# Host-packed weight loads, and low parts of the down weights on POOL with its own walk over the experts

## The reference, cut to what matters

```python
a = RMSNorm(h); proj = a @ w_in               # z | x,B,C | dt | u,v
h += concat(ssd(z, xBC, dt), gmlp(u, v)) @ w_out
h += HierMoE(RMSNorm(h))                      # the best of 4 groups, then the best 2 of its 4 experts
h += sigmoid(RMSNorm(h) @ w_pg) * RMSNorm(p @ w_ple)
y = RMSNorm(h)

# HierMoE, for each expert e of 16 (1024 -> 512 -> 1024):
hid = silu(t @ w_gate[e]) * (t @ w_up[e])
y = y + comb[:, e:e+1] * (hid @ w_down[e])
```

## Time and profile before

| | |
|---|---|
| median of three runs | 1130.89 us |
| the profiled execution | 1131.93 us |
| its span, from the first to the last instruction | 1130.1 us |
| PE busy | 1057.6 us, 94% |
| DVE busy | 700.2 us, 62% |
| ACT busy | 502.7 us, 44% |
| POOL busy | 184.1 us, 16% |
| moved by DMA | 204.82 MB, mean 181 GB/s |

### The profile page before, as it was taken

One profiled execution on the slowest core, in us unless ns is written; L12 is line 12 of the kernel. 1 busy time (PEld: TensorE's weight loads), 2 busy tenths in 40 slices (PEclk: granted clock), 3 DMA queues, 4 the chain that ended last, 5 costly groups with the idle time before them and its releaser, 6 DMA issues.

```text
span 1130.1 us, 17444 instructions
## 1 busy us (share of the span) xinstructions
PE 1057.6 (94%) x6221; PEld 912.5 (81%) x6222; DVE 700.2 (62%) x1103; ACT 502.7 (44%) x872; POOL 184.1 (16%) x344
## 2 busy tenths in 40 slices
PE   7999999997999999946999999799999999999896
PEld 5777799985776788745988999798899999878685
DVE  4422575814767667156599467889946753585664
ACT  6733322123111121151589357788935652564332
POOL 3611001100133112111000000000000000065542
PEclk9999999999899999857999999999999999999999
DMA  9701400222512362169399775999977556142441
GB/s 335 233 23 55 170 2 1 75 79 72 164 70 76 120 234 85 56 195 296 141 367 380 266 278 179 381 358 369 380 265 278 181 190 225 53 171 75 169 149 56
DMA packets 131607, 204.82 MB, mean 181 GB/s; under 512 B 11375, under 2 KB 98031, under 8 KB 131434
## 3 DMA queue, kind: packets, MB, share of 16 engines
q1 hardware_dynamic: 121450, 169.82, 44.2%
q0 software_dynamic: 6512, 21.77, 5.4%
q10 hardware_dynamic: 3600, 12.62, 2.8%
HBM read 169.74 MB, written 34.46 MB: 181 GB/s over the span
## 4 chain that ended last, share of the span: by engine, by line
PE 56%; DVE 10%; issue 4%; DMA 3%; ACT 2%; DVEq 1%; POOL 0%; ACTq 0%; SPq 0%; POOLq 0%; another core or an unknown queue 0%
PE bank L608 12%; PE bank L610 11%; PE bank L609 11%; PE bank L602 4%; DVE w_lo L1531 3%; PE bank L852 3%; PE bank L854 3%; PE bank L853 3%; PE bank L596 2%; PE bank L824 1%; PE bank L791 1%; DMA raw_gu<-in_w_up 1%; ACT w_hi L1923 1%; DMA xg<-m_rows,index_u 1%; DMA hx<-h_rows 1%
## 5 line engine op out<-in xcount | busy, mean ns | idle before, releaser
L608 PE MATMUL bank<-w_hi,xh 128*128 128x256 f32 x768 | 220.2, 287 | 2.7 <-DVE xl L1052 2.7
L609 PE MATMUL bank<-w_lo,xh 128*128 128x256 f32 x768 | 218.0, 284 | 0.0
L610 PE MATMUL bank<-w_hi,xl 128*128 128x256 f32 x768 | 218.0, 284 | 0.0
L1531 DVE SCALAR_TENSOR_TENSOR w_lo<-raw_gu,cols,w_hi 128x512 fp32r<-128x512 f32 x264 | 177.9, 746 | 10.9 <-ACT w_hi L1923 9.8
L1923 ACT ACTIVATE w_hi<-raw_gu,cols 128x512 fp32r<-128x512 f32 x264 | 165.4, 714 | 32.1 <-PE bank L610 16.4
L608 PEld LDWEIGHTS bank<-w_hi,xh 128*128 128x128 f32 x768 | 147.7, 192 | 4.2 <-issue 3.1
L609 PEld LDWEIGHTS bank<-w_lo,xh 128*128 128x128 f32 x768 | 147.9, 193 | 0.8
L610 PEld LDWEIGHTS bank<-w_hi,xl 128*128 128x128 f32 x768 | 147.7, 192 | 0.0
L608 PE MATMUL bank<-w_hi,hid_hi 128*128 128x512 f32 x192 | 79.6, 415 | 0.0
L2231 POOL COPY index_u<-token_u 128x1 uint32 (+1 forms) x25 | 6.1, 244 | 434.2 <-PE bank L602 411.5
L609 PE MATMUL bank<-w_lo,hid_hi 128*128 128x512 f32 x192 | 75.9, 395 | 0.0
(11 more groups left out here) (373 smaller groups left out, 2169.2 us busy)
## 6 DMA issues: line engine op xcount, KB each, us to landing
raw_gu<-in_w_gate SPq DMA_DIRECT2D x32, 1024.0 KB, 7.6
raw_gu<-in_w_up SPq DMA_DIRECT2D x32, 1024.0 KB, 10.1
raw_d<-in_w_down SPq DMA_DIRECT2D x16, 2048.0 KB, 11.8
y_rows<-yb ACTq DMA_DIRECT2D x24, 512.0 KB, 6.3
raw_w<-in_w_in SPq DMA_DIRECT2D x20, 512.0 KB, 6.3
xr<-in_x_prompt_t SPq DMA_DIRECT2D x8, 512.0 KB, 9.4
xst<-in_x_prompt SPq DMA_DIRECT2D x8, 512.0 KB, 9.7
raw_o<-in_w_out SPq DMA_DIRECT2D x8, 512.0 KB, 3.5
```

The costliest lines, as they stand in the source:

```text
L608: nc.tensor.matmul(out, lh(k), rh(k), start=(k == 0), stop=False)
L609: nc.tensor.matmul(out, lh(k), rl(k), start=False, stop=False)
L610: last = nc.tensor.matmul(out, ll(k), rh(k), start=False, stop=(k == (K or len(ks)) - 1))
L1531: ins = V.scalar_tensor_tensor(out=gu_lo[:, k, :, cols_], in0=raw_gu[q // KC][:, k, :, :], scalar=gain(e, k), in1=gu_hi[:, k, :, cols_].bi ...
```

## The change

Five things are changed.

- The host lays the weights out in the order of the buffers. w_in is loaded in runs of 4 KB, gate and up as four quarters of 1 MB in runs of 8 KB, down as two halves of 1 MB in runs of 8 KB. ACT waits for each quarter or half instead of each half or the whole.
- The low parts of the down weights are made by POOL, four passes (`d_low`), counted by the semaphore d_split. PE waits for d_split by halves, and `hid_transposes(1)` goes behind the first quarter of the down products.
- POOL walks the experts by `each_block`: in each block it gathers the next rows, and in a block with splits it then runs `d_low` of the next expert.
- The low parts of the second half of w_out are made by POOL (semaphore o_low); ACT's `decay(0)` comes after the first of its four high passes of that half.
- The fill with ones covers the 16 blocks that may be unused, always, and is issued right after the third w_in block's loads; the loads of p_in and ple_row come before the wait for the plan, that of ps_in before the loop over the experts.

The core of the diff:

```diff
@@ SP
+            for b in range(NE, BLOCKS):
+                sp.dma_start(y_rows[b * P:(b + 1) * P, :].rearrange("p (k n) -> p k n", n=P),
+                             ones[:, :].unsqueeze(1).to_broadcast([P, KC, P])).then_inc(s("unused_filled"), 16)
...
+                sp.dma_start(raw_gu[q][:, part * KC // 2:(part + 1) * KC // 2].rearrange("p k w n -> p (k w n)"),
+                             i["w_gate_up"][bass.ds(e, 1), q, part].rearrange("o p n -> p (o n)")).then_inc(s(f"w{2 * q + part}_loaded"), 16)
...
             def next_expert(e):
-                done = sp.snap(STEPS * e)
-                gate_up(e, 0, sp.snap(done - KC - DC))
-                gate_up(e, 1, sp.snap(done - DC))
-                down(e, done)
+                done = sp.snap(GU_STEPS * e)
+                for q in range(2):
+                    for part in range(2):
+                        gate_up(e, q, part, sp.snap(done - (3 - 2 * q - part) * KC // 2))
+                down(e, 0, sp.snap(DC * e - DC // 2))
+                down(e, 1, sp.snap(DC * e))
@@ PE, one_block
                 b_rows(pe.snap(16 * n + 16))
-                hid_transposes(1, pe.snap(2 * n + 1))
-                pe.wait_ge(s("w_split"), steps + STEPS)
+                pe.wait_ge(s("d_split"), d_steps + DC // 2)
...
                 for quarter in range(4):
                     part, half = quarter // 2, quarter % 2
+                    if quarter == 2:
+                        pe.wait_ge(s("d_split"), d_steps + DC)
+                    if quarter == 1:
+                        hid_transposes(1, pe.snap(2 * n + 1))
@@ DVE
             front(0)
-            for j in range(KC // 2):
-                o_split(1, j)
             weights(0)
...
-                if more and splits:
-                    split(e + 1, "D0")
                 if more:
                     b_hid(dve.snap(n + 1), 0)
-                if more and splits:
-                    split(e + 1, "D1")
@@ POOL
+            for j in range(KC // 2):
+                pool.wait_ge(s("a_high"), KC * 5 + KC // 2 + j + 1)
+                G.tensor_tensor(wo_lo[1][:, j, :], raw_o[:, j, :], wo_hi[1][:, j, :].bitcast(F32), ALU.subtract).then_inc(s("o_low"), 1)
...
-            gather(0, None, None)
-            total = blocks_in_all(pool)
-            with pool.Fori(0, total) as b:
+            def d_low(e):
+
+                done = STEPS * e if isinstance(e, int) else pool.snap(STEPS * e)
+                for k in range(DC):
+                    pool.wait_ge(s("w_high"), done + 2 * KC + k + 1)
+                    G.tensor_tensor(d_lo[:, k, :], raw_d[:, k, :], d_hi[:, k, :].bitcast(F32), ALU.subtract).then_inc(s("d_split"), 1)
+
+            def one_block(b, e, splits, more):
+
                 n = pool.snap(b + 1)
                 gather(n, n, pool.snap(16 * n))
+                if splits and more:
+                    d_low(e + 1)
+
+            gather(0, None, None)
+            d_low(0)
+            each_block(pool, one_block)
```

More of the change, by code:

```diff
@@ L61, in build @@
     TILES = NT + 1
-    IN = i["w_in"].shape[2]
+    IN = sizes["w_in"][2]
     HEADS = i["dt_bias"].shape[1]
@@ L525, in _ @@
                     sp.wait_ge(s("out_done"), 2 * TILES)
-                    down(0, None)
+                    for part in range(2):
+                        down(0, part, None)
+                if n == TILES + 1:
+                    sp.wait_ge(s("mTp_done"), TILES)
+                    sp.wait_ge(s("h_stored"), 16 * TILES)
+                    sp.dma_start(p_in, i["p_prompt_t"].rearrange("(k p) t -> p k t", p=P)).then_inc(s("p_loaded"), 16)
+                    sp.dma_start(ple_row, i["norm_ple"].partition_broadcast(P).rearrange("q o n -> q (o n)")).then_inc(s("c_rows_loaded"), 16)
@@ L528, in _ @@
             sp.wait_ge(s("plan_ready"), 1)
             total = blocks_in_all(sp)
[L530 to L535, removed]
@@ L536, in next_expert @@
-            def next_expert(e):
-                done = sp.snap(STEPS * e)
-                gate_up(e, 0, sp.snap(done - KC - DC))
-                gate_up(e, 1, sp.snap(done - DC))
-                down(e, done)
[L542 to L546, removed]
+            def next_expert(e):
+                done = sp.snap(GU_STEPS * e)
+                for q in range(2):
+                    for part in range(2):
+                        gate_up(e, q, part, sp.snap(done - (3 - 2 * q - part) * KC // 2))
+                down(e, 0, sp.snap(DC * e - DC // 2))
+                down(e, 1, sp.snap(DC * e))
@@ L557, in _ @@
-            sp.wait_ge(s("w_split"), STEPS * NE)
-            sp.dma_start(raw_d[:, 0:PC, :], i["w_ple"][0].rearrange("(k p) n -> p k n", p=P)).then_inc(s("d_loaded"), 16)
+                for part in range(2):
+                    sp.wait_ge(s("w_split"), GU_STEPS * NE - (3 - 2 * q - part) * KC // 2)
+                    sp.dma_start(raw_gu[q][:, part * KC // 2:(part + 1) * KC // 2].rearrange("p k w n -> p (k w n)"),
+                                 i["w_pg_rows"][q, part]).then_inc(s(f"w{2 * q + part}_loaded"), 16)
@@ L1525, in split @@
                 done = STEPS * e if isinstance(e, int) else dve.snap(STEPS * e)
-                steps = SPLITS[at]
-                for q in steps:
+                for q in SPLITS[at]:
                     dve.wait_ge(s("w_high"), done + q + 1)
[L1529 to L1534, removed]
-                        ins = lo(d_lo[:, ks, :], raw_d[:, ks, :], d_hi[:, ks, :])
-                    ins.then_inc(s("w_split"), 1)
+                    k, cols_ = q % KC, slice(q // KC * HE, (q // KC + 1) * HE)
+                    V.scalar_tensor_tensor(out=gu_lo[:, k, :, cols_], in0=raw_gu[q // KC][:, k, :, :], scalar=gain(e, k),
+                                           in1=gu_hi[:, k, :, cols_].bitcast(F32), op0=ALU.mult, op1=ALU.subtract).then_inc(s("w_split"), 1)
             def final_ple(k):
@@ L1608, in _ @@
             b_xT(1)
-            for part in ("B", "D0", "D1"):
-                split(0, part)
+            split(0, "B")
             b_hid(1, 0)
@@ L1886, in _ @@
             bt_evict(0)
-            for j in range(KC // 2):
+            o_high(1, 0)
+            decay(0)
+            for j in range(1, KC // 2):
                 o_high(1, j)
-            decay(0)
             for n in range(TILES + 2):
@@ L2327, with quarters @@
         arrays["state_ssm"][0].reshape(sizes["state_ssm"][1], -1, sizes["state_ssm"][4]).transpose(2, 0, 1))
+    w_in = arrays.pop("w_in")[0]
+    ssd, conv, heads, gm = sizes["ssd_norm"][1], sizes["conv_w"][2], sizes["dt_bias"][1], sizes["gmlp_norm"][1]
+    first = [ssd + conv + heads, ssd + conv + heads + gm, ssd + BANK, ssd, 0]
+    arrays["w_in_blocks"] = np.ascontiguousarray(
+        np.stack([w_in[:, c:c + BANK].reshape(-1, 2, p, BANK).transpose(0, 2, 1, 3) for c in first]))
+    arrays["w_in_dt"] = np.ascontiguousarray(w_in[:, ssd + conv:ssd + conv + heads].reshape(-1, p, heads).transpose(1, 0, 2))
+    n_e, de = sizes["w_gate"][1], sizes["w_gate"][3]
+    def quarters(pair):
+        both = np.stack(pair, axis=-2)
+        both = both.reshape(both.shape[:-3] + (2, d // p // 2, p, 2, 2, both.shape[-1] // 2))
+        both = np.moveaxis(both, (-2, -6, -4, -5, -3, -1), (-6, -5, -4, -3, -2, -1))
+        return np.ascontiguousarray(both.reshape(both.shape[:-3] + (-1,)))
+    arrays["w_gate_up"] = quarters((arrays.pop("w_gate")[0], arrays.pop("w_up")[0]))
+    w_pg = arrays.pop("w_pg")[0]
+    arrays["w_pg_rows"] = quarters((w_pg[:, :BANK], w_pg[:, BANK:]))
+    w_down = arrays.pop("w_down")[0].reshape(n_e, 2, de // p // 2, p, d)
+    arrays["w_down_rows"] = np.ascontiguousarray(w_down.transpose(0, 1, 3, 2, 4).reshape(n_e, 2, p, -1))
     arrays["p_prompt_t"] = np.ascontiguousarray(arrays.pop("p_prompt")[0, 0].T)
```

95 lines of the change are left out of this document (43 added, 52 removed).

## The result

The changed kernel takes 1326.7 us (median of four runs, 1319.63 to 1328.99) against 1131.22 us: a ratio of 1.1702, 95% interval 1.1666 to 1.1738. The profiled execution has a span of 1327.3 us, 197.2 us more than before. All but 5.6 us of this lie between the experts' first product and the last transposes of gathered rows: from 526.30 to 1173.67, 647.4 us, against 455.8 us.

The account below looks back on a forecast made before the run. PE was taken as the bound, busy 94% of the span. From the profiled 1131.93 us, -15.2 + 166.5 - 2.5 gave 1280.7; as that run is 1.04 us above the median, 1280 us, range 1207 to 1335.

Parts of the forecast that it names:

- PE's waits for these gathers: Sign: among PE's waits, one of about 130 us in all at L602 for the gather.
- the stalled blocks: Sign: 15 blocks of 28 to 30 us, the others 18.6.
- the late gathers: Sign on POOL: in 15 places the gather is issued some 20 us after the one before, behind four passes.
- The stall: PE waits 8.6 us for rows gathered behind d_low, plus 2.5 us half clock: 11.1 us, 15 times, +166.5.
- the landing: Time from the late gather's issue until its rows arrive: 6.4 us taken, from 4.1 / 7.5 / 8.0 (least, median, longest).
- the pass: One POOL d_low pass over 128x1024: 1.89 us, taken from the norm's multiplication; four make 7.56 us.
- The sg waits: PE's seven waits for gated hidden rows, 12.6 us, and 2.6 us of clock behind the long one go: -15.2 us.
- The start of the experts: First gather could land faster (-3.6 us), but d_low(0) runs beside DVE's eight low passes (+1.5 us): 0 taken.
- o_split: Second half of w_out's low parts moves from DVE to POOL, halving PE's 4.9 us wait for dec: -2.5 us.
- The fill, the w_in runs, the order on SP: Earlier fill of y_rows, w_in in 4 KB runs (at most 3.4 us back) and SP's changed loads: 0 taken.
- The second rival's lock: POOL's passes hold DVE's A0 passes; with gathers in time, 3.2 us in each of nine blocks: 1143 us, chance 0.05.
- The first rival: d_low ends before the gather is missed, needing under 0.4 us a pass; only gains left: 1113 us, chance 0.05.

Follow-up runs that it names:

- the two kernels above: Changed kernel with down weights' low parts on DVE and p_in, ps_in, ple_row loads mid-loop on SP: 1126.17 us; with gate and up in 1 KB runs too: 1125.35 us.
- the third experiment: Changed kernel with its order kept, but d_low of experts 1 to 15 covering 64 of 1024 columns: 1263.1 us (1.1170).

## Why the prediction was right, and where its sizes were off

The forecast was 149 us slower, 166.5 of stalls less some gains; 195 us were measured, so that 1326.7 us lies near the upper end of the range, 1335. The mechanism is the one that happened: the gather queued behind `d_low`, in 15 places. Undoing that one order takes 152 us back. Of the signs named, PE's waits for these gathers came to 175.3 us and not 130, and the stalled blocks to 28.65 to 34.71 us and not 28 to 30; the late gathers were issued 32 to 40 us after the one before, not 20. By steps:

- **The stall, forecast 11.1 us, measured 13.6.** In the same pair of blocks, 12 and 13, counted from the end of block 12's down products: `d_low` starts 5.3 us later (4.9 forecast); the four passes take 10.3 us and not 7.9; from their end to the issue 0.9 and not 1.2; the landing is 9.2 and not 6.4; PE is ready 11.9 us after (11.7). The wait is 13.9 us, not 8.6. Over the 15 places a stall cost 13.6 us with the clock. The nine places where DVE's A0 passes follow average 13.3 us; in the six others passes of 2.4 us, with no A0 pass beside them, and shorter landings give 9.3. The clock cost 1.9, not 2.5.
- **The mis-sized terms are the pass and the landing.** The nearest row was a multiplication with one of its inputs broadcast from a single column; with two full inputs a pass takes 2.33 to 2.43 us even where DVE does not meet it. The Trainium skill gives a price for just this ("GPSIMD Engine Reference", section on elementwise work, side-by-side cycle accounting): a two-input add over 2048 elements takes 4497 ns on GpSimd, so half of it would be 2.25 us (an estimate from that figure). The traces, with 2.33 to 2.43 us, agree with it rather than with the row that was taken. Meeting DVE adds 0.9 us to the four passes (10.3 against 9.4 us), where 0.3 was allowed. The landing was put below its median because the loads were thought to be over; but `d_low`'s end itself releases the next load, and in the nine places DVE's A0 passes release another. In the six the average of 6.2 us is about what was taken.
- **The sg waits, -15.2:** gone; within the experts 204.3 us of stalls made the stretch 191.6 us longer, so -12.7 with all else, 0.8 of a slower first block and a floor of 18.66 in place of 18.59 us a block included. It is what is left over, not measured by itself. The reason given for the long one, p_in's place, is not enough, as the two kernels above show.
- **The start of the experts, 0:** from the gather's issue to the first product 15.9 us and not 12.4, so +3.5. The first landing did fall to 4.7 us, but `d_low(0)` and DVE's passes met for longer than the +1.5 that was allowed: a single one of DVE's was held for 10.26 us.
- **o_split, -2.5:** the first product at L824 came 1.3 us earlier and the product with w_out 0.3; taking the edit back made no difference. The low bound is also mis-added: the wait and a half-clock stretch are 4.9 + 2.65, some 7.5 us and not 7.0.
- **The fill, the w_in runs, the order on SP, 0:** nothing seen, and none was taken back by itself. Up to the first gather the changed kernel is 1.3 us later, less than the spread among the profiles of its variants (their planner's first matmul is at 490.5 to 494.6 us).
- **The second rival's lock** is real. DVE's late passes cost nothing here, as forecast, because they lay inside PE's wait; only the 0.9 us by which POOL's own passes grew counts. Where the gather is in time the lock decides, at 5.9 and not 3.2 us a block. Its row was read too simply: the DVE pass of 3.09 us ends at 326.86, 0.55 us after the last of four POOL passes of about 1.03 us each, and began during the second of them. It was held through more than one, so the row bears out that the two contend, but not that the second waits for a single instruction.
- **The first rival** was asked for less than it needs: four passes under 0.4 us would not do, as the third experiment shows.

## What to carry to other kernels

A queue is a promise to everyone behind it: before giving an idle engine more work, list what else it issues and whether the new work waits for something later than that. Look at the place in the queue before the busy share: POOL idled in most of the span and its queue was still what PE waited for. And where a wait of about 1 us recurs behind a nearly full engine, try the order of its queue before moving work off it: here this took 10 us off one kernel, and nothing off another whose waits stood elsewhere.

## What the runs showed of the hardware that was not expected

- How DVE and POOL hold each other up differs from place to place. The view of the tile w_lo in the changed kernel (shortest, median and longest pass in ns, first and last start):

```profile
L1524 DVE SCALAR_TENSOR_TENSOR w_lo<-raw_gu,cols,w_hi x264: 735/746/10259, 510.1 to 1179.7; 128x512 fp32r<-128x512 f32 x132
...
L2231 POOL TENSOR_TENSOR w_lo<-raw_d,w_hi x64: 2328/2414/2852, 511.9 to 1126.7; 128x1024 fp32r<-128x1024 f32 x64
```

  One DVE pass took 10.26 us: at the start of the experts it began 0.5 us before the first of four POOL passes that ran one right behind the other, and was held until all four were through. In the nine stalls with A0 passes the two take turns instead: two passes of DVE's take 2.8 to 2.9 us each, and two of POOL's 2.8 us. Either way, a held DVE pass ends 0.55 us after a POOL pass does (521.64 after 521.09, 613.13 after 612.58; 19 held passes in all). What decides which of the two happens was not found.
- In the changed kernel a gather of 128 rows lands in 4.2 to 4.7 us while no load is under way, in 5.3 to 7.9 us beside halves of the down weights, and in 7.8 to 9.5 us in the nine places where a 1 MB load of gate and up is issued beside it as well. The runs of those gate and up loads (1 KB or 8 KB) make no difference to it: 8.6 and 8.8 us on average.
